# Gate and branch products of the merge stage: page steps fall between runs of products instead of between single ones

## The reference

```python
y_fox = o_fox.reshape(B, S, W_FOX) @ w_br_fox          # 512 -> 1024
y_dil = o_dil.reshape(B, S, W_DIL_OUT) @ w_br_dil      # 256 -> 1024
merged = jax.nn.sigmoid(gate_fox) * y_fox + jax.nn.sigmoid(gate_dil) * y_dil
return merged @ w_mix_out
```

## Time and profile before

| | |
|---|---|
| median of 3 runs | 2645.4 us (2644.33 to 2645.79) |
| span of the profiled execution | 2644.8 us |
| PE busy over the span | 2606.2 us, 99% |
| DVE, ACT, POOL busy | 44%, 20%, 7% |
| gate products, first and last start | 682.4 and 1246.1 us |
| page steps of the fox sample attention | 798.8 to about 1116 us |
| page steps of the dil sample attention | about 1119 to 1236 us |

### The profile page before, as it was taken

One profiled execution on the slowest core, in us unless ns is written; L12 is line 12 of the kernel. 1 busy time (PEld: TensorE's weight loads), 2 busy tenths in 40 slices (PEclk: granted clock), 3 DMA queues, 4 the chain that ended last, 5 costly groups with the idle time before them and its releaser, 6 DMA issues.

```text
span 2644.8 us, 37539 instructions
## 1 busy us (share of the span) xinstructions
PE 2606.2 (99%) x14274; PEld 1810.4 (68%) x14274; DVE 1151.7 (44%) x2814; ACT 527.8 (20%) x1163; POOL 178.0 (7%) x284
## 2 busy tenths in 40 slices
PE   8999999999999999999999999999999999999999
PEld 7655566666656666676445676558888888888887
DVE  2255653332253333343551123346666666654432
ACT  2233323222202222121011112321212112110002
POOL 1000002232102222000000000000000000000000
PEclk9999999999999999999999999999999999999999
DMA  5000101100118888786205003533544352152201
GB/s 197 23 13 10 61 1 59 61 20 23 46 29 257 250 255 255 227 268 233 106 32 191 32 0 108 162 91 115 165 144 150 131 178 65 36 201 93 66 30 68
DMA packets 207161, 294.49 MB, mean 111 GB/s; under 512 B 20781, under 2 KB 145086, under 8 KB 205942
## 3 DMA queue, kind: packets, MB, share of 16 engines
q1 hardware_dynamic: 148150, 187.76, 21.9%
q10 hardware_dynamic: 42976, 89.26, 10.5%
q0 software_dynamic: 15856, 15.07, 2.3%
HBM read 268.07 MB, written 63.35 MB: 125 GB/s over the span
## 4 chain that ended last, share of the span: by engine, by line
PE 95%; DMA 2%; ACT 1%; DVE 1%; ACTq 1%; issue 1%; SPq 0%; DVEq 0%
PE psum L2701 21%; PE psum L3083 11%; PE psum L1063 10%; PE psum L2043 8%; PE psum L531 5%; PE psum L2385 4%; PE psum L2131 4%; PE psum L1419 3%; PE psum L2232 3%; PE psum L2051 3%; PE psum L702 3%; PE psum L719 2%; PE psum L2359 2%; PE psum L1435 2%; PE psum L1455 2%; PE psum L730 1%
## 5 line engine op out<-in xcount | busy, mean ns | idle before, releaser
L2701 PE MATMUL psum<-arena 128*128 128x272 f32 x2464 | 567.0, 393 | 0.1
L2701 PEld LDWEIGHTS psum<-arena 128*128 128x128 f32 x2464 | 469.3, 191 | 97.1 <-issue 0.2
L3083 PE MATMUL psum<-arena 128*128 128x256 f32 (+1 forms) x1584 | 288.1, 356 | 0.0
L1063 PE MATMUL psum<-arena 128*128 128x512 f32 (+3 forms) x960 | 284.7, 458 | 0.0
L2043 PE MATMUL psum<-arena 128*128 128x368 f32 (+1 forms) x768 | 280.4, 477 | 0.9 <-DVE arena L1979 0.7
L3083 PEld LDWEIGHTS psum<-arena 128*128 128x128 f32 (+1 forms) x1584 | 252.4, 178 | 34.7 <-issue 3.2
L1063 PEld LDWEIGHTS psum<-arena 128*128 128x128 f32 (+1 forms) x960 | 150.2, 179 | 89.1 <-issue 78.3
L2043 PEld LDWEIGHTS psum<-arena 128*128 128x128 f32 x768 | 128.4, 191 | 52.6 <-issue 15.6
L2804 DVE TENSOR_TENSOR arena<-arena,psum 128x272 f32<-128x272 f32 (+2 forms) x330 | 111.8, 377 | 112.8 <-PE psum L2701 112.0
L1419 PEld LDWEIGHTS psum<-arena 128*128 128x128 f32 x848 | 105.1, 141 | 69.6 <-issue 45.4
L2825 DVE SCALAR_TENSOR_TENSOR arena<-arena 128x1024 f32<-128x1024 f32 x88 | 113.1, 1285 | 52.6 <-ACT arena L2727 51.1
(11 more groups left out here) (265 smaller groups left out, 2900.3 us busy)
## 6 DMA issues: line engine op xcount, KB each, us to landing
arena<-in_cache_fox_kv ACTq DMA_DIRECT2D x128, 256.0 KB, 4.7
arena<-in_cache_fox_kv SPq DMA_DIRECT2D x128, 256.0 KB, 5.0
out_win_s<-in_cache_win_kv ACTq DMA_DIRECT2D x8, 4080.0 KB, 15.5
arena<-in_w_up SPq DMA_DIRECT2D x44, 512.0 KB, 6.6
arena<-in_w_down SPq DMA_DIRECT2D x14, 1408.0 KB, 6.4
arena<-in_cache_win_kv SPq DMA_DIRECT2D x16, 1024.0 KB, 8.5
arena<-in_cache_mem_kv SPq DMA_DIRECT2D x16, 1024.0 KB, 6.3
arena<-in_w_in SPq DMA_DIRECT2D x9, 1024.0 KB, 8.0
```

What stands on the lines that cost most here:

```text
L1063: last = pe.matmul(banks[c0 // 512][p0:p0 + r, 0:n], xn_tile(k, g, t), wD[g][:, k, w0:w0 + n], start=(k == 0), stop=(k == KD - 1))
L2701: last = pe.matmul(bank_of(j, x, p), w[:, k, :], r[:, k, Q4 * p:Q4 * p + Q4], start=(k == 0), stop=(k == 3))
L3083: last = pe.matmul(down_out(u)[p0:p0 + r, 0:n], hT(f)[:, tok + t * P:tok + t * P + r], slot[slots[c]][:, f - fa, c0:c0 + n], start=(f == f ...
```

## The change

Gate products are asked for in two runs of four, and the two or four branch products of a unit in one run. Each run is due when its first product was due before. What each product computes, its waits and its semaphores are as before, and so are all yields of the other engines.

```diff
                 for k in range(KD):
-                    yield gate_due(u) + (gate_due(u + 1) - gate_due(u)) * k / (KD + kn)
+                    if k % 4 == 0:
+                        yield gate_due(u) + (gate_due(u + 1) - gate_due(u)) * k / (KD + kn)
                     if k == 0:
...
                 for k in range(kn):
-                    yield gate_due(u) + (gate_due(u + 1) - gate_due(u)) * (KD + k) / (KD + kn)
+                    if k == 0:
+                        yield gate_due(u) + (gate_due(u + 1) - gate_due(u)) * (KD + k) / (KD + kn)
```

## The result

The changed kernel takes 2665.7 us (median of 4 runs, 2661.2 to 2671.3) against 2644.9 us before (4 runs, the three of the table ahead and one more, 2641.7 to 2645.8): 20.9 us more, a ratio of 1.0085 with a 95% interval of 1.007 to 1.010. The profiled execution has a span of 2664.8 us, 20.0 us more than before.

What follows compares the result with a forecast made beforehand. PE's own list, busy 2606.2 of 2644.8 us, was taken as the bound. 2644.8 + 25.8 (waits for copies) + 1 (ACT's blocks) - 1 (page waits) = 2670.6, forecast 2671 us, range 2652 to 2693 us.

Steps and rivals of the forecast that it cites:

- Changes of kind: PE's list: about 280 fewer changes from one kind of piece to another gain 0 to 3 us, taken as 0.
- The rival in which batches pay: PE loses time wherever the kind of piece changes, so runs win it back: 2638 us, chance 0.05.
- Waits for copies: Sample attentions: grouped steps on PE wait for DVE's and ACT's copies, 17.8 us fox, 10.4 us dil, 25.8 us added.
- The signs: Changed trace, 798 to about 1275 us: PE idle some 38 us, at named copy lines; a four-product run takes 2.47 us.
- ACT's blocks: Loads on ACT's list keep it from copying and meet groups of T more often: 0 to 5 us, taken as 1.
- Page waits: PE's waits for value pages at V, with the lower clock behind them: -7.7 to +10 us, taken as -1.
- the waits for the tanh: Gates stage: the tanh comes no later, since its products end earlier in PE's list; 0 us.
- Fewer waits than counted: Still slower, but part of the copy waits is hidden; at half the price +13 us, 2658 us, chance 0.15.
- Page waits and clock: V and K come in bursts, pages are late and the clock drops: 24 us beside the sum, 2695 us, chance 0.12.
- No change: Copies are in time after all, or page waits and changes of kind win back the loss: 2647 us, chance 0.04.
- faster: The rival in which batches pay: 25 us gained from 280 changes against 18 us of waits, 2638 us, chance 0.05.

Runs made afterwards that it cites:

- the last experiment: Kernel before with only the gate weights' loads moved from ACT's list to SP's: ratio 0.9989; with value page spacing also halved: 0.9981.

## Why the prediction was right, and where its sizes were off

**The bound and the place.** PE's list was the time, and the loss is in the gates stage, 467.0 against 449.7 us. Of the 20.0 us between the two spans 17.3 are there and 0.2 ahead of it; the other 2.5 us stand behind the stage, where the profiled kernels scatter by some 4 us (1396.4 us from the stage's end to the last instruction before, 1398.9 after, 1400.3 with the branch runs alone), so no cause is sought for them.

**Changes of kind cost next to nothing.** Right within the 0 to 3 us that were given: in runs of two, two products with their T and P take what they take when they alternate, and four products in the changed kernel take 2.47 us, four times the 0.62 us of one. The rival in which batches pay falls. The rule of the Trainium skill behind it, that matmuls run back-to-back in batches ("Perfetto Trace Analysis", Matmul Optimizations), had nothing to give in this stage: the alternating stretches already ran at a granted clock of 1.00 or 0.99, and the change left it at 1.00. Over the whole stage a small gain is possible. Its length less all idle time in brackets, 0.16 us for each of them and the time lost to the lower clock is 449.7 - 11.9 - 2.1 - 3.4 = 432.3 us before and 467.0 - 25.3 - 9.4 - 1.7 = 430.6 us after, so that the 280 changes may have been worth some 2 us, 0.01 us each.

**Waits for copies.** The mechanism held, and its counts nearly. In the fox sample attention 12 S waited for DVE as counted; 13 T, as against 12 counted; and 13 P as against 14. In start-to-start terms, bracket plus 0.16 us each, S took 4.6 + 12 x 0.16 = 6.5 us (6.7 counted), T without the block named below 4.8 + 12 x 0.16 = 6.7 us (6.0 counted: after a copy by DVE a third T costs 0.59, not 0.50 us), and P 3.7 + 13 x 0.16 = 5.8 us (5.1 counted). Together 19.0 us where the count had 17.8. The dil sample attention has S 4.1 us in 8 waits, T 1.4 us in 4, P 0.6 us: 6.1 + 13 x 0.16 = 8.2 us; counted were 10.4 us, with a last V in them. The short copies confirm the part of T and S in the fox sample attention by an experiment; for P and the dil sample attention the traces alone speak. The 1.38 us that the prediction read at 1226 us from a T to the S behind its copy are the 1.38 us at 811 us after the change.

**The signs.** The granted clock of the stage is 1.00, a run of four products takes 2.47 us, and PE waits at the lines that were named. One sign was put wrongly: PE's idle time should have gone from 12.3 to some 38 us, and it is 26.6 us. The prediction added waits from start to start to idle time that is shown 0.16 us shorter for each; for 51 waits for copies that is 8 us. Most of the rest is page waits that went.

**ACT's blocks.** 1 us was taken from a range of 0 to 5. The block of the earlier trace rows is there again, at 888 us of the changed kernel, as all engines in order of time show:

```profile
888.00 1.83 ACTq L2015 DMA_DIRECT2D arena<-in_w_in  x1
889.81 1.04 PE L1419 MATMUL psum<-arena 128*128 128x128 f32 x8
889.86 2.14 ACTq L2016 DMA_DIRECT2D arena<-in_w_br_fox  x1
...
893.18 0.60 ACT L1485 ACTIVATE arena<-psum 128x512 f32<-128x512 f32 x1 [7.41 <-issue]
893.88 0.37 ACTq L1677 DMA_DIRECT2D arena<-in_cache_fox_kv  x1
893.93 1.08 PE L1419 MATMUL psum<-arena 128*128 128x128 f32 x4 [2.02 <-ACT arena L1485]
```

It is now 2.02 us instead of 1.51, and the piece behind it takes 1.08 us instead of 0.63: the clock fell, and the stretch from 870 to 910 us has a granted clock of 0.96, 1.6 us. Beside it stand 1.3 us of brackets at three units whose gate products waited for the tanh (L2044 for L2083 and L2085) against 0.3 us before, which the prediction had put at nothing.

**Page waits: the term that was mis-sized.** The prediction took -1 us from a range of -7.7 to +10. The changed kernel won nearly the whole of the lower end in the fox sample attention: behind the first T, 5.0 us of waits became 0.6, and the two stretches with a lower clock, 3.4 us (0.65 from 936.7 to 941.6 us and 0.66 from 1049 to 1054 us), went with them. The fox sample attention therefore grew by 12.8 us, though its waits for copies alone take 19.0 us. In the dil one 3.2 us of waits for pages and requests became 1.3 us, and it grew by 4.4 us. These are 5.0 - 0.6 + 3.4 + 3.2 - 1.3 = 9.7 us less where 1 was taken, and the dil waits for copies came 2.2 us short of their count. Against that stand the waits of the fox steps (1.2 us over their count), the block of ACT's list with its clock (1.1 us over the 1 us taken), the waits for the tanh (1.0 us) and the stretch behind the stage (2.5 us). The forecast was 5.8 us too high for the span and 5.3 us for the median; it is that near because errors of both signs cancel in part. What removed the page waits stays open: a stage 4% longer leaves the loads more time, but the kernel with only the gate products in runs was nearly as long and kept 4.0 us of them (though it ran at 1.00 from 798 to 1262 us), and the one with short copies kept 1.9 us. With landing times of 2.5 to 9.1 us a microsecond either way may decide for two V, but no run shows it. A range was the right form for this term, and no row of the trace before pointed to its lower end. The early value pages show that a page wait isn't simply a gain left lying: they trade with ACT's blocks.

**The rivals.** Fewer waits than counted (2658 us) had the mechanism wrong, since the counted waits came in full and other waits went. Page waits and clock (2695 us) went the other way. No change (2647 us) and faster (2638 us) fall with a ratio whose interval begins at 1.007. That the clock can matter is shown by the kernel with the gate products alone in runs, by 7.8 us, but behind the stage.

## What to carry to other kernels

Where single matrix products stand between steps that hand their result to another engine, they are the cover of the copies, and here that alternation cost next to nothing on PE (1.058 us for a product and a T, the sum of the two). Gathering the products into runs gathers the steps too, and the waits can be counted from the new order beforehand: a step that starts less than 1.38 us after the T whose copy it needs pays the difference, every time. The whole change in time is less sure than this count, since other waits move with it. A limit for a run follows from the buffers: with two turn banks, two T in one go don't wait for each other, and runs of two kept it to that. Before a transfer is moved to another queue or asked for earlier, count what is queued behind the request: 1.1 us a page on a queue with two streams, or a block of 5.6 us ahead of a copy, cost more than the waits that were to be removed.

## What the hardware showed that was not expected

In the kernel with only the gate products in runs the granted clock fell to 0.57 for 19 us in which PE was busy 18.4 us, behind a stretch at 1.00. The changed kernel has nearly the same waits ahead of the same 96 products (0.78, 0.62, 0.89 and 0.87 us within 20 us, against 0.78, 0.62, 0.89 and 0.84 us) and runs them at 1.00, in 10.9 us. It doesn't happen in every run of that kernel: the stretch alone loses 0.43 x 19 = 8 us of clock, and the run of 2659.3 us, with a mean granted clock of 0.998, lost some 5 us in all. What decides it stays open. Waits of 2.3 us, of 2.0 us (893 us, above) and of 2.8 us (early value pages) were followed by a lower clock (0.65 over 4.9 us, 0.66 from 893 to 898 us, 0.72 from 890 to 896 us), one of 1.5 us was not; but at 1277 us of the kernel before a transpose (L369) waited 2.95 us and the granted clock of the next 6 us was 1.00. So the length of a wait alone doesn't tell.

The scatter between runs of one kernel goes with this clock. Of the 21 runs of the kernel before that stand beside the last experiment, the three with a mean granted clock of 0.994 took 2648.6 to 2652.8 us, and the four with 0.998 or 0.999 took 2638.7 to 2643.8 us.
